# Expert rows gathered for two experts at a time, squares and roots of the expert norms one stage earlier, in a one-core forward pass

## The chip, the core and the metric

One core of a Trainium2 chip runs the whole program as a single launch. The metric is the device time of one execution in microseconds. The trace gives, for one execution, every instruction of the five engines (PE is TensorE, PEld its weight loads, DVE is VectorE, ACT is ScalarE, POOL is GpSimd) and every transfer, which SP (SyncE) issues except for a few.

## What is computed

Two networks follow each other on 256 tokens of width 1024, all in float32. The first block (mixer, memory attention, hierarchical experts) is not touched. The second has two layers. Layer 0 mixes with a state-space scan (SSD), layer 1 with attention, and each ends in an expert-choice stage:

```python
def moe_ec(h, router_w, w1, w3, w2):
    cap = EC_CAPACITY * T // N_EXPERTS_2
    aff = jax.nn.softmax(logits, axis=-1)
    gate, idx = lax.top_k(jnp.swapaxes(aff, 1, 2), cap)
    xg = h[bidx, idx]
    a = jnp.einsum('becd,edf->becf', xg, w1)
    g = jnp.einsum('becd,edf->becf', xg, w3)
    y = jnp.einsum('becf,efd->becd', jax.nn.silu(a) * g, w2)
    y = y * gate[..., None].astype(y.dtype)
    return jnp.zeros_like(h).at[bidx, idx].add(y.astype(h.dtype))
...
x = x + g2l * moe_ec(rmsnorm(x, norm2_w[i]) * (1.0 + sc2l) + sh2l, ...)
```

Each of 16 experts picks its 32 best rows (cap) of 256. Its three matrices are 1024 by 1024, so a layer reads 16 x 3 x 4 MB, some 201 MB. In layer 0 the tokens and a context of 256 rows go through the experts (two streams), in layer 1 the tokens alone. A last rmsnorm gives the output.

## The kernel before

The kernel is written out by hand: every engine has its own instruction list in each block, with semaphores between them, and a barrier of all five engines stands between blocks. A block is a stage: the SSD stage, the expert stage of layer 0 (tiles end in e or e0), the attention stage (5), the expert stage of layer 1 (e1). The two expert stages are one function, `expert_choice(l)`.

**Weights.** A list `stream` fixes the order in which SP issues the loads; SP takes them in that order and waits before each until the piece that held the buffer is used up (`piece.before.freed`). Buffers are six slots of 2 MB and extra tiles. An expert is six pieces of 2 MB (two halves each of w1, w3, w2). Layer 0 has 7 buffers (slots 0 to 5, `extra0`), layer 1 has 9 (two of them made of two tiles each, `extra1` with C and `extra2` with hT). In the SSD stage the slots also serve as scratch; all six become free with the last matmul of its output product (`scratch_use`), so the first pieces of layer 0 are issued there. In the attention stage four pieces of layer 1 are loaded while it runs, and five at or after its end.

**Front of an expert stage.** `NormT` normalises: ACT squares each tile of 128 rows with a row sum (`scalar_squares`), POOL makes the root of each (`pool`, `root`), DVE scales the tile (`vector_scale`), PE transposes it, DVE and ACT bring it to hT with gain and bias. Four tiles in layer 0, two in layer 1. Then come router logits, softmax, the choice of 32 rows by expert on DVE (`top8`), one-hot matrices (`mark`), and `fetch`: matmuls of the normalised rows (stationary, 128 x 128) with one-hot columns gather the chosen rows, transposed, into `xgT`. `take_unit` brings them out of PSUM. In layer 1 PE first runs four matmuls that only keep it busy, `hold(pe, 4)`.

**The expert loop.** `GROUP = 4`: rows are gathered for four experts at once, so a gather matmul has 4 x 32 = 128 moving columns. The first group is gathered in front of the loop; in each of experts 0 to 11 a quarter of the next group's gather follows the first product (`fetch(psum[2], ...)`), with ACT taking it out. PE's list for expert e is: two halves of w1 (line 2898), transposes of the gates, fetch, two halves of w3, scatter of the previous expert, transposes, two halves of w2.

Of the kernel before, what the change touches and what calls it, by code (L numbers as in the profile page):

```python
# [168 lines left out]
def build(nc, A, out):  # L169
# [15 lines left out]
    with ctx:  # L185
# [31 lines left out]
        dve_step, act_step, pool_step = sem("dve_step"), sem("act_step"), sem("pool_step")  # L217
# [116 lines left out]
        moe2_weights(0, (0, 1, 2, 3, 4, 5, SLOTS))  # L334
        ring.last[SLOTS + 1] = ring.last[SLOTS + 2] = extra_room[1]
        ring.last[SLOTS + 3] = extra_room[2]
        for n in (0, 1, 2):
            weights(("qkv", n), [(0, KD, 512, rows("attn_qkv_w_2")[:, :, n * 512:(n + 1) * 512])], (n + 5) % SLOTS)
        for n in range(2):
            weights(("attn_out", n), [(0, 4, D, rows("attn_out_w_2")[:, 4 * n:4 * n + 4, :])])  # L340
        moe2_weights(1, (4, 5, 0, 1, 2, 3, SLOTS + 1, SLOTS + 2, SLOTS + 3))
# [14 lines left out]


# [55 lines left out]
        counted = {"streams": 0, "norms": 0, "head_norms": 0, "ada": 0}  # L413

        class NormT:


            def __init__(self, tag, srcs, xn, hT, gain_col, bias_col=None, cols=None, apart=False, by=(DVE, ACTE)):
# [6 lines left out]
                counted["streams"] += self.T  # L425
                counted["norms"] += 1
# [6 lines left out]
            def pool(self, pool):  # L433
                for t in range(self.T):
                    pool.wait_ge(squared, self.before + t + 1)
                    root(pool, t, 1, D, rooted)

# [13 lines left out]
            def tensor(self, pe):  # L451
                m = self.per_bank()
                opened = [banks.open((self.tag, n), self.by[n % 2]) for n in range(KD // m)]
                for t in range(self.T):
                    pe.wait_ge(normed, self.before + t + 1)
# [1592 lines left out]
        with ExitStack() as ssd:  # L2048
            Yt_base = (nc.sbuf_base + 31) // 32 * 32
            Yt = sb("Yt", [P, 16, TT * P], scope=ssd)  # L2050
            Yt_r = nc.alloc_sbuf_tensor_at("Yt_r", [P, 16, TT * P], F32R, offset=Yt_base)
            rowsB = sb("rowsB", [P, 2, HPG, TT * P], scope=ssd)
            xst = sb("xst", [P, 2, 3, GW], scope=ssd)
# [31 lines left out]
            pos[0] = late + 2080  # L2085
            y_high_late = carve(8 * 512, flat_r).rearrange("p (c n) -> p c n", c=8)
            y_high = lambda i: h_high[:, i, :] if i < 8 else y_high_late[:, i - 8, :]
# [3 lines left out]
            g1 = rows_flat[:, 0:2048].rearrange("p (s n) -> p s n", s=2)  # L2091
            part = xst[:, :, :, :].rearrange("p d t n -> p (d t n)")[:, 0:1024].rearrange("p (a n) -> p a n", a=2)
# [45 lines left out]
            def _(pe):  # L2138
# [143 lines left out]

                sum_squares(6)
# [1068 lines left out]
```

## Time and profile before

| | us |
|---|---|
| median of 3 runs (2228.2 to 2230.95) | 2229.8 |
| the profiled execution, its own time | 2231.04 |
| its span in the trace | 2229.2 |
| PE busy | 2030.7 (91%) |
| DVE busy | 972.8 (44%) |
| ACT busy | 648.5 (29%) |
| POOL busy | 72.4 (3%) |
| 16 DMA queues, mean rate | 280 GB/s |

The mean over the span hides the stages. In the page's row of 40 slices (55.7 us each), the DMA rate is 427 or 428 GB/s in most slices of the two expert stages and 77 to 139 in the SSD stage. PE's granted clock is 0.977 of full speed in the mean.

### The profile page before, as it was taken

What the parts mean: (1) busy time and instruction counts of PE and PEld (TensorE: products, weight loads), DVE (VectorE), ACT (ScalarE), POOL (GpSimd) and SP (SyncE); (2) the same over time, 40 slices, a digit from 0 to 9 for tenths busy, and PEclk for the clock granted to TensorE, in tenths of its full rate; (3) what the DMA queues carried; (4) which work ended last, traced back from release to release, by engine and by line L of the source; (5) the groups of instructions that cost most, each with busy time, mean ns of one, the idle gap of its engine ahead of it and who ended that gap; (6) DMA issues with size and microseconds to landing.
All of it is one profiled execution on the core that took longest, in us unless ns stands there. A gap on an engine that the chain in (4) does not pass through costs nothing. (4 is left out here: it accounts for less than half of the span.)

```text
span 2229.2 us, 25119 instructions
## 1 busy us (share of the span) xinstructions
PE 2030.7 (91%) x10198; PEld 1076.0 (48%) x10198; DVE 972.8 (44%) x1668; ACT 648.5 (29%) x1284; POOL 72.4 (3%) x106
## 2 busy tenths in 40 slices
PE   6987988999899999999899999988899899999887
PEld 5844444444377888878643333322445422222222
DVE  4687224444688889882522221222466400011002
ACT  4244023111276667762211111100226111111000
POOL 0101010000000000000100000000120000000000
PEclk9999998999999999999999999999999999999999
DMA  8637477899333433322489999999820599999997
GB/s 289 214 139 277 176 266 294 339 388 384 111 97 98 139 105 114 114 96 77 186 360 429 427 428 427 427 428 428 328 110 1 211 427 427 424 427 426 427 425 301
DMA packets 147177, 623.58 MB, mean 280 GB/s; under 512 B 15443, under 2 KB 66134, under 8 KB 109046
## 3 DMA queue, kind: packets, MB, share of 16 engines
q1 hardware_dynamic: 142144, 601.65, 67.8%
q0 software_dynamic: 2352, 16.91, 1.9%
q10 hardware_dynamic: 2566, 3.41, 0.5%
q8 instruction: 82, 1.34, 0.2%
q14 instruction: 33, 0.27, 0.0%
HBM read 620.76 MB, written 1.18 MB: 279 GB/s over the span
## 5 line engine op out<-in xcount | busy, mean ns | idle before, releaser
L2898 PE MATMUL bank<-slots,xgTe 128*64 128x512 f32 (+1 forms) x1584 | 355.0, 595 | 30.4 <-DMA slots<-in_moe_w 30.3
L3119 DVE TENSOR_TENSOR actse<-sge,bank 32x512 f32<-32x512 f32 (+1 forms) x48 | 32.8, 682 | 499.2 <-PE bank L2898 278.4
L2898 PEld LDWEIGHTS bank<-slots,xgTe 128*64 128x64 f32 (+1 forms) x1584 | 102.7, 125 | 259.5 <-issue 216.2
L2898 PE MATMUL bank<-slots,aTe 128*64 128x512 f32 (+1 forms) x800 | 188.4, 615 | 18.3 <-issue 18.3
L514 PE MATMUL bank<-slots_r 128*128 128x512 f32 x512 | 201.2, 393 | 0.0
L3016 ACT ACTIVATE sge<-bank 32x512 f32<-32x512 f32 (+1 forms) x48 | 28.3, 590 | 481.5 <-PE bank L2898 481.3
L513 PE MATMUL bank<-hT_r,slots_r 128*128 128x512 f32 x384 | 155.6, 405 | 0.0
L515 PE MATMUL bank<-slots_r 128*128 128x512 f32 x384 | 152.0, 396 | 0.0
L583 PE MATMUL bank<-slots,hT 128*128 128x512 f32 (+1 forms) x320 | 133.2, 578 | 4.6 <-DVE hT L480 3.0
L2898 PEld LDWEIGHTS bank<-slots,aTe 128*64 128x64 f32 (+1 forms) x800 | 55.3, 128 | 130.8 <-issue 130.8
L514 PEld LDWEIGHTS bank<-slots_r 128*128 128x128 f32 x512 | 96.3, 188 | 22.6
L3028 ACT ACTIVATE aTe<-bank 128x512 f32<-128x512 f32 x32 | 19.1, 597 | 275.4 <-PE bank L2955 275.4
L583 PEld LDWEIGHTS bank<-slots,hT 128*128 128x128 f32 x320 | 61.7, 194 | 74.5 <-issue 66.9
L2493 DVE SCALAR_TENSOR_TENSOR slots<-slots,vcols 128x512 f32<-128x512 f32 x128 | 95.5, 751 | 4.0 <-ACT slots L2345 0.3
L1690 PE MATMUL bank<-slots,hT 128*64 128x512 f32 x368 | 88.4, 615 | 9.6 <-ACT hT L1802 4.9
L2133 DVE TENSOR_TENSOR slots_r<-slots,slots_r 128x2048 fp32r<-128x2048 f32 x32 | 73.1, 2286 | 42.4 <-ACT slots_r L2128 42.2
L515 PEld LDWEIGHTS bank<-slots_r 128*128 128x128 f32 x384 | 72.2, 188 | 17.7
L513 PEld LDWEIGHTS bank<-hT_r,slots_r 128*128 128x128 f32 x384 | 72.1, 188 | 16.8 <-issue 1.2
L2362 ACT ACTIVATE rowsB<-rowsB,nb 128x128 f32<-128x128 f32 x256 | 76.5, 391 | 2.2 <-DVE rowsB L2619 2.2
L362 POOL TENSOR_SCALAR rstd<-eps_rows 128x1 f32<-128x1 f32 (+5 forms) x41 | 17.6, 430 | 1796.9 <-ACT xn L430 624.3
L2128 ACT ACTIVATE slots_r<-slots 128x2048 fp32r<-128x2048 f32 x32 | 61.0, 1906 | 51.1 <-PE bank L515 51.1
L2898 PE MATMUL bank<-extra0e,xgTe 128*32 128x512 f32 (+1 forms) x304 | 68.8, 594 | 4.5 <-DMA extra0e<-in_moe_w 4.5
(561 smaller groups left out, 3099.0 us busy)
## 6 DMA issues: line engine op xcount, KB each, us to landing
slots<-in_moe_w SPq DMA_DIRECT2D x149, 2048.0 KB, 26.5
slots<-in_ada_w SPq DMA_DIRECT2D x24, 2048.0 KB, 12.2
extra0e<-in_moe_w SPq DMA_DIRECT2D x23, 2048.0 KB, 26.5
slots<-in_ssd_in_w SPq DMA_DIRECT2D x48, 512.0 KB, 5.3
slots<-in_moe_w_gate SPq DMA_DIRECT2D x23, 1024.0 KB, 10.6
slots<-in_moe_w_up SPq DMA_DIRECT2D x23, 1024.0 KB, 12.6
slots<-in_moe_w_down SPq DMA_DIRECT2D x23, 1024.0 KB, 7.3
rowsB<-acum_rows POOLq DMA_DIRECT2D x16, 1024.0 KB, 5.8
```

The lines of the kernel that those rows point to most:

```text
L513: pe.matmul(out, lhsT[0], rhs[1], start=start, stop=False, skip_group_check=True)
L514: pe.matmul(out, lhsT[0], rhs[0], start=False, stop=False, skip_group_check=True)
L515: return pe.matmul(out, lhsT[1], rhs[0], start=False, stop=stop, skip_group_check=True)
L583: i = pe.matmul(b.ap[:, 0:width], lhsT(k), rhs(k), start=(k == 0), stop=(k == K - 1))
L1690: i = pe.matmul(b.ap[j * CAP1:(j + 1) * CAP1, :].rearrange("p (m n) -> p m n", m=2), xg[:, p // 2 % 2, k, at:at + CAP1], piece.ap.rearrang ...
L2128: act.activation(high_half(w), raw_half(w), ACT.Copy).then_inc(w_rounded, 1)
L2133: dve.tensor_tensor(low_half(w), raw_half(w), high_half(w).bitcast(F32), ALU.subtract).then_inc(w_split, 1)
L2362: i = act.activation(r, r, ACT.Exp, bias=nb[:, t, col:col + 1])
L2493: i = dve.scalar_tensor_tensor(o, padded[:, c, :, j:j + S], tap(j, CH(g)[c]), o, ALU.mult, ALU.add)
L2898: i = pe.matmul(bank[64 * n:64 * n + NJ * CAP, :], lhsT(4 * h + k), wv[:, 0, n * 512:(n + 1) * 512], start=(h == 0 and k == 0), stop=(h == ...
L3016: i = act.activation(sg[r_, :], psum[0][r_, :], ACT.Silu)
L3119: i = dve.tensor_tensor(acts[r_, :], sg[r_, :], psum[1][r_, :], ALU.mult)
```

## The change

`GROUP` goes from 4 to 2 in both layers, so a gather matmul has 64 moving columns and each gather takes twice as many of them for the same rows; fourteen experts carry a share of the next group's gather, where twelve did. The squares and roots of the expert norms move to the end of the block in front (`early_squares`, `early_roots`, with a third POOL instruction for the factor of 32). The scaling is shared: DVE takes the even tiles of a stream and ACT the odd ones (`shared_scale`). Layer 0 has a norm for each stream. Scratch of the SSD stage moves out of slots 3 to 5, so that three pieces of layer 0 may be loaded before the output product ends; the order of buffers is changed with it. In layer 1 one buffer lies where the attention's queries were and is free once these are transposed; `fin`, the last norm's gain, has a tile of its own.

```diff
@@ end_scratch, group_scratch, gate_scratch
-        scratch_use = Piece(None, None, 0, None)
+        group_scratch, gate_scratch, end_scratch = (Piece(None, None, 0, None) for _ in range(3))
         for slot in range(SLOTS):
-            ring.last[slot] = scratch_use
+            ring.last[slot] = (end_scratch, end_scratch, end_scratch, gate_scratch, group_scratch, group_scratch)[slot]
...
-        moe2_weights(0, (0, 1, 2, 3, 4, 5, SLOTS))
-        ring.last[SLOTS + 1] = ring.last[SLOTS + 2] = extra_room[1]
+        moe2_weights(0, (5, 4, 3, 0, 1, 2, SLOTS))
+        ring.last[SLOTS + 1] = extra_room[1]
...
-        moe2_weights(1, (4, 5, 0, 1, 2, 3, SLOTS + 1, SLOTS + 2, SLOTS + 3))
+        queries_room = Piece(None, None, 0, None)
+        ring.last[SLOTS + 2] = queries_room
+        moe2_weights(1, (1, 2, 5, 4, SLOTS + 2, 3, 0, SLOTS + 1, SLOTS + 3))
...
+        def stream_root(pool, t, done):
+            link = chain(pool, pool_step)
+            c = slice(t, t + 1)
+            link(pool.tensor_scalar(rstd[:, c], eps_rows[:, c], float(D * EPS), None, ALU.add))
+            link(pool.tensor_tensor(rstd[:, c], rstd[:, c], minus_half[:, 0:1], ALU.pow))
+            pool.tensor_scalar(rstd[:, c], rstd[:, c], float(D) ** 0.5, None, ALU.mult).then_inc(done, 1)
+        def early_squares(act, junk, tiles):
+            for t, src in enumerate(tiles):
+                act.wait_ge(stream_added, counted["added"] + 1)
+                if t:
+                    act.wait_ge(squared, counted["streams"] + t)
+                counted["added"] += 1
+                act.activation(junk, src, ACT.Square, accum_out=eps_rows[:, t:t + 1]).then_inc(squared, 1)
+        def early_roots(pool, n):
+            for t in range(n):
+                pool.wait_ge(squared, counted["streams"] + t + 1)
+                stream_root(pool, t, rooted)
...
+            def shared_scale(self, eng, by):
+                for t, src in enumerate(self.srcs):
+                    if (t % 2 == 0) != (by == DVE):
+                        continue
+                    eng.wait_ge(rooted, self.before + t + 1)
+                    dst = self.xn[:, t, :].rearrange("p (h j m) -> p h m j", h=2, j=4)
+                    src = src.rearrange("p (h m j) -> p h m j", h=2, j=4)
+                    r = rstd[:, self.at + t:self.at + t + 1]
+                    if by == DVE:
+                        eng.tensor_scalar(dst, src, r, None, ALU.mult).then_inc(normed, 1)
+                    else:
+                        eng.activation(dst, src, ACT.Copy, scale=r).then_inc(act_normed, 1)
...
-            GROUP = 4
+            GROUP = 2
...
-                norm = NormT(tag, [r for rs in res for r in rs], xn, hT, segs, apart=True)
+                norms = [NormT(f"{tag}s{j}", res[j], xn[:, NT * j:NT * (j + 1), :], hT[:, :, S * j:S * (j + 1)], segs_of(j),
+                               at=NT * j, shared=True) for j in range(NJ)]
...
-                    norm.pool(pool)
...
-                    norm.scalar_squares(act)
-                    norm.evacuate(act, ACTE)
+                    for norm in norms:
+                        norm.shared_scale(act, ACTE)
+                    for norm in norms:
+                        norm.evacuate(act, ACTE)
```

ACT at the border between the SSD stage and the expert stage of layer 0, before (C and X are the two streams, the UNCONDITIONAL_BRANCH rows are the border):

```order
L2382 ACTIVATE slots_r<-Yt,vcols 128x512 x2
L2048 UNCONDITIONAL_BRANCH
L2993 UNCONDITIONAL_BRANCH [waits barrier_Pool_Activation_PE_DVE_SP_release]
L430 ACTIVATE xne,eps_rows<-C 128x1024 x2
L430 ACTIVATE xne,eps_rows<-X 128x1024 x2
L484 ACTIVATE hT<-bank,modcol,ncol 128x256 [waits bank_full]
```

The same place on ACT in the changed kernel:

```order
L2440 ACTIVATE hT_r<-Yt,vcols 128x512 x2
L376 ACTIVATE hp,eps_rows<-C 128x1024 [waits stream_added]
L376 ACTIVATE hp,eps_rows<-C 128x1024 [waits squared,stream_added]
L376 ACTIVATE hp,eps_rows<-X 128x1024 [waits squared,stream_added] x2
L2101 UNCONDITIONAL_BRANCH
L3060 UNCONDITIONAL_BRANCH [waits barrier_Pool_Activation_PE_DVE_SP_release]
L481 ACTIVATE xne<-C,rstd 128x2x128x4 [waits rooted]
L481 ACTIVATE xne<-X,rstd 128x2x128x4 [waits rooted]
L537 ACTIVATE hT<-bank,modcol,ncol 128x256 [waits bank_full]
```

The four squares now stand ahead of the border, the last of them behind the last addition to the streams, and two scalings stand behind it.

PE in expert 0 of layer 0, before: the product with w1 (from xgTe), the gate transposes (gcure), the gather for the next group (from hT and xne, into one PSUM bank), the product with w3:

```order
L2898 MATMUL bank<-slots,xgTe 64x512 [waits slot_loaded1,emptied_by_act,emptied_by_dve]
L2898 MATMUL bank<-slots,xgTe 64x512 x7
L2937 MATMUL bank<-consts,gcure 128x128 [waits emptied_by_act,gc_ready_e0]
L2937 MATMUL bank<-consts,gcure 128x128
L2871 MATMUL bank<-hT,xne 128x128 [waits onehot_ready_e0,emptied_by_dve]
L2871 MATMUL bank<-hT,xne 128x128 x7
L2898 MATMUL bank<-slots,xgTe 64x512 [waits slot_loaded2,emptied_by_act]
```

The same place on PE in the changed kernel:

```order
L2966 MATMUL bank<-slots,xgTe 64x512 [waits slot_loaded4,emptied_by_act,emptied_by_dve]
L2966 MATMUL bank<-slots,xgTe 64x512 x7
L3005 MATMUL bank<-consts,gcure 128x128 [waits emptied_by_act,gc_ready_e0]
L3005 MATMUL bank<-consts,gcure 128x128
L2939 MATMUL bank<-hT,xne 128x64 [waits onehot_ready_e0,emptied_by_dve]
L2939 MATMUL bank<-hT,xne 128x64 x15
L2966 MATMUL bank<-slots,xgTe 64x512 [waits slot_loaded3,emptied_by_act]
```

Eight gather matmuls of 128 columns became sixteen of 64, between the same neighbours.

## Rows read from the trace of the kernel before

**Rows 1.** Windows: stretch, length, busy us of each engine, PE clock, DMA share, GB/s

```profile
1091.00:1134.00 43.00, 31.94 (x189) 21.86 (x190) 27.43 (x67) 14.84 (x30) 5.60 (x8) 0.88 0.83 342
...
1500.00:1560.00 60.00, 51.05 (x242) 16.84 (x238) 12.68 (x20) 3.73 (x10) 0.00 (x0) 1.00 1.01 428
...
1700.00:1750.00 50.00, 45.84 (x192) 23.14 (x188) 19.36 (x52) 14.05 (x34) 0.00 (x0) 1.00 0.00 1
```

**Rows 2.** Timeline of PE, experts of layer 0: start us, us, what, idle before

```profile
1130.06 7.09 PE L2898 MATMUL bank<-slots,xgTe 128*64 128x512 f32 x32
...
1345.12 3.60 PE L2898 MATMUL bank<-extra0e,xgTe 128*64 128x512 f32 x16
1349.60 3.65 PE L2898 MATMUL bank<-slots,xgTe 128*64 128x512 f32 x16 [0.87 <-DMA slots<-in_moe_w]
...
1577.20 3.65 PE L2898 MATMUL bank<-slots,aTe 128*64 128x512 f32 x16
```

**Rows 3.** Timeline of SP's issues of weight loads

```profile
1057.75 0.37 SPq L354 DMA_DIRECT2D slots<-in_ssd_out_w  x1
...
1091.19 3.01 SPq L354 DMA_DIRECT2D slots<-in_moe_w  x6
...
1133.75 24.09 SPq L354 DMA_DIRECT2D slots<-in_moe_w  x6
...
1749.34 0.81 SPq L354 DMA_DIRECT2D slots<-in_moe_w  x2
...
1778.78 22.13 SPq L354 DMA_DIRECT2D slots<-in_moe_w  x6
```

**Rows 4.** Timeline of all engines, front of the expert stage of layer 0

```profile
1092.04 0.69 DVE L2732 TENSOR_TENSOR X<-X,xst 128x512 f32<-128x512 f32 x1
1094.63 1.06 ACT L430 ACTIVATE xne<-C 128x1024 f32<-128x1024 f32 x1 [22.53 <-PEq L2048]
...
1096.17 0.57 POOL L363 TENSOR_TENSOR rstd<-rstd,minus_half 128x1 f32<-128x1 f32 x1
...
1098.14 4.79 PE L460 MATMUL bank<-consts,xne 128*128 128x128 f32 x24 [6.98 <-DVE xne L445]
...
1102.00 1.34 DVE L445 TENSOR_SCALAR xne<-X,rstd 128x1024 f32<-128x1024 f32 x1 [0.33 <-POOL rstd L363]
1103.40 1.09 PE L460 MATMUL bank<-consts,xne 128*128 128x128 f32 x8 [0.46 <-DVE xne L445]
...
1121.09 9.04 PE L2871 MATMUL bank<-hT,xne 128*128 128x128 f32 x64 [1.30 <-DVEq L3093]
```

**Rows 5.** The same timeline, front of the expert stage of layer 1

```profile
1750.14 0.69 DVE L3316 TENSOR_TENSOR X<-X,part 128x512 f32<-128x512 f32 x1
...
1751.37 3.67 PE L509 MATMUL bank<-consts 128*128 128x512 f32 x8 [2.07 <-PEq L3173]
...
1756.84 1.10 PE L460 MATMUL bank<-consts,xne 128*128 128x128 f32 x8 [0.91 <-DVE xne L445]
```

**Rows 6.** Timeline of PE: a gather of layer 0, a 32-column matmul elsewhere, and their successors

```profile
1137.35 1.95 PE L2871 MATMUL bank<-hT,xne 128*128 128x128 f32 x16
1139.23 7.09 PE L2898 MATMUL bank<-slots,xgTe 128*64 128x512 f32 x32
```

```profile
627.48 1.97 PE L2254 MATMUL bank<-slots,consts 128*128 128x32 f32 x16
629.29 0.68 PE L2259 MATMUL bank<-slots,consts 128*128 128x256 f32 x2
```

**Rows 7.** PE behind an earlier border of blocks: its timeline, and the window

```profile
1589.25 3.13 PE L2042 MATMUL bank<-consts,modcol 128*128 128x128 f32 x16 [1.91 <-PEq L2755]
```

```profile
1590.00:1592.00 2.00, 2.00 (x12) 2.00 (x10) 0.63 (x1) 2.00 (x5) 1.29 (x3) 0.50 1.03 400
```

**Rows 8.** Timeline of PE, experts 11 and 15 of layer 1

```profile
2074.06 3.63 PE L2898 MATMUL bank<-slots,xgTe 128*32 128x512 f32 x16 [1.18 <-DMA slots<-in_moe_w]
...
2201.75 3.63 PE L2898 MATMUL bank<-slots,xgTe 128*32 128x512 f32 x16 [1.17 <-DMA slots<-in_moe_w]
```

More of the change, by code:

```diff
@@ L454, in tensor @@
                 for t in range(self.T):
-                    pe.wait_ge(normed, self.before + t + 1)
+                    self.wait_normed(pe, t)
                     for n, b in enumerate(opened):
@@ L2281, in _ @@
                     outputs(g)
+                group_scratch.freed = (emptied[DVE], banks["y", SSD_G - 1, 1].done)
                 sum_squares(6)
@@ L2286, in _ @@
                 sum_squares(7)
+                gate_scratch.freed = (bank_full, banks["ss", 7].full)
                 outs = [(t, n, banks.open(("so", t, n), DVE)) for t in range(TT) for n in range(2)]
@@ L2311, in _ @@
                     half(w).freed = (gate_full, q + 1) if q < 7 else (bank_full, b.full)
-                scratch_use.freed = (bank_full, b.full)
+                end_scratch.freed = (bank_full, b.full)
             @block.gpsimd
@@ L2825, in _ @@
                         hold(pe, 4)
-                    norm.tensor(pe)
+                    for norm in norms:
+                        norm.tensor(pe)
                     pe.wait_ge(wide_ready, 1)
@@ L2994, in _ @@
                 def _(act):
-                    norm.scalar_squares(act)
-                    norm.evacuate(act, ACTE)
+                    for norm in norms:
+                        norm.shared_scale(act, ACTE)
+                    for norm in norms:
+                        norm.evacuate(act, ACTE)
                     act.wait_ge(sub_ready, 1)
@@ L3040, in _ @@
                     dve.tensor_copy(wide[:, :, 0:N_EXP], wr).then_inc(wide_ready, 1)
-                    norm.vector_scale(dve)
-                    norm.evacuate(dve, DVE)
+                    for norm in norms:
+                        norm.shared_scale(dve, DVE)
+                    for norm in norms:
+                        norm.evacuate(dve, DVE)
                     b = banks[tag, "quarters"]
@@ L3198, in build @@
             q_ready, k_ready = sem("q5_ready"), sem("k5_ready")
+            X_tiles = [X[:, t, :] for t in range(NT)]
             to_qT = Transpose("qT5", lambda n, t: q[:, t, n * P:(n + 1) * P], QH // 2, P, lambda g, m: qT[:, g:g + m, :])
@@ L3239, in _ @@
                 to_qT.wait_all(pe)
+                queries_room.freed = (bank_full, banks["qT5", to_qT.groups()[-1][0]].full)
                 for g in (KVH - 2, KVH - 1):
```

77 lines of the change are left out of this document (53 added, 24 removed).

## The prediction

> **What bounds the kernel now.** I read the stages by window first, since the means of the page mix them. In the expert stages the transfers run at 428 GB/s with the engines' share at 1.01, and a few stretches are poor: the last 50 us of attention move 1 GB/s, and the 43 us between the end of the SSD stage and the first used piece of layer 0 move 342 [rows 1]. So transfers bound the expert stages, and what counts is when they start to run without a gap.
>
> The timeline of SP's issues says when. In layer 0 seven pieces go out at and just after 1091.19, the eighth at 1133.75, when expert 0 has used its first piece [rows 3]. Seven pieces at 4.91 us each (2.10 MB at 427 GB/s) end near 1127, so the transfers then stand still for some 7 us: the window's 43 x (1 - 342/427) = 8.6 us says the same. In layer 1 the steady stream starts at 1778.78, again with the first freed buffer [rows 3]. I call these two moments the starts. **All buffers are full at both starts**, before as after, so a start depends on the chain norm, router, choice, gather, and not on how early the first pieces came.
>
> The timeline of PE tells the rest. From expert 0 at 1130.06 to expert 8 at 1345.12 PE runs without a wait for a transfer: 26.88 us per expert. The first such wait comes at 1349.60, and the last product ends at 1577.20 + 3.65 = 1580.85 [rows 2], 450.8 us after expert 0 began. Six pieces take 6 x 4.91 = 29.5 us. So PE has 2.6 us per expert in hand, no more. In layer 1 it reaches the transfers only in expert 11 [rows 8].
>
> **The sum, term by term.**
>
> *A, front of layer 0: -2.9 us.* The last addition ends at 1092.04 + 0.69 = 1092.73, ACT's first square starts at 1094.63 [rows 4]: the barrier waited for SP, whose six issues end at 1091.19 + 3.01 = 1094.20 [rows 3], and then took 0.4. Now three of the six are issued near 1058, behind the last load of the SSD stage [rows 3], and the other three end by 1092.7. But the last square (1.06 and 0.19 for the read of the sum) and three POOL instructions (two like the 0.57 one at most [rows 4], one of some 0.2, with 0.1 between) now stand ahead of the barrier: 1092.8 + 1.25 + 1.1 + 0.4 = 1095.6, a border 1.0 later. Behind it DVE scales two tiles in place of four, ACT two beside it (a row of ACT's square, the same size, takes 1.06), so both end near 1099 where DVE ended at 1102.00 + 1.34 = 1103.34. PE becomes the limit: 24 transposes took 4.79 at the lower clock, eight 1.09 [rows 4]; 32 from 1097.6 end near 1103.1 against 1104.49. The first stream is brought to hT meanwhile, so the half of that work which came after the last transpose goes: together 2.6 earlier. The one-hot marks for two experts in place of four save some 0.3. The first gather has the same 64 records [rows 4]; at 64 columns they cost what they did (term B), so nothing there. Bounds: 0 (ACT slow on its permuted writes, or the low clock for longer) and -4.4: the first gather's 64 records took 9.04 [rows 4], where 64 at the steady 0.118 of term B are 7.5, so 1.5 more if it now runs at full clock throughout.
>
> *B, experts of layer 0: +1.8 us.* The gather of an expert is 16 records (a float32 matmul leaves two) in 1139.23 - 1137.35 = 1.88 us, 0.118 each with 128 columns. The nearest narrow row has 32 columns and the same full stationary: 16 in 629.29 - 627.48 = 1.81, 0.113 each [rows 6]. A quarter of the columns saves 4%, so 64 columns save nothing to speak of and 16 more records cost 1.85 us per expert. PE's own pace becomes 26.88 + 1.85 = 28.73 for fourteen experts and 25.0 for the two without a gather: 452.2 us, against the 450.8 that transfers allowed. The transfers themselves: the third piece of expert 0 was freed 9.05 us after the start; now 10.9, and two pieces take 9.8, so they wait 1.1 once. The two limits lie within half a microsecond of each other, +1.4 and +1.1; where both bind by turns the end comes a little behind either, hence +1.8. Bounds: +1.1 (PE never late) and +6 (0.3 us more per expert over fourteen: a stretch of lower clock or a wait for ACT, which now takes out eight small blocks where it took four).
>
> The Trainium skill (TensorE: Matmul & The Clock Gate, section "Back-to-back issue gap") gives the gap of an isolated warm matmul as moving columns over 2.4 GHz plus 2.5 ns, by which half the columns would be nearly half the price and the gather would cost no more than before. Its section on LDWEIGHTS ties the weight load to the stationary's columns, which stay 128, and the rows here side with that one. By the first, B would be +0 and the sum of all terms near zero or below; by the rows it is +1.8.
>
> *Attention stage: 0.* It keeps its instructions; ACT and POOL are idle where squares and roots go, except behind the last addition. Its weights follow the same pieces as before. One more piece (4.9 us of transfer) comes in during the 50 us that move nothing [rows 1]. That work would show only if the start waited for transfers: of its nine pieces five are issued from 1749.34 on [rows 3], 24.6 us of transfer, which end near 1774, ahead of the start at 1778.78; now four of them do.
>
> *C, front of layer 1: +2.5 us.* Here the barrier waited for the last addition alone: 1750.83, PE's next matmul at 1751.37 [rows 5]. Square and root now stand between, 1.25 + 1.1 + 0.1 = 2.4 us. Behind the border PE must first run the four holding matmuls, 3.67 us; they lay beside squares, roots and scaling, and that cover is gone. Transposes of the second tile began at 1756.84; now 1751.37 + 2.4 + 3.67 + 1.05 = 1758.5, 1.65 later [rows 5]. PE also idles 4.5 us there where it idled 2.07. Behind another border it idled 1.91 us and the next 2 us had the clock at 0.50, that is 1.2 GHz of 2.4 [rows 7]; a spell of that in the holding matmuls can cost at most 1.85, half of what runs in it, and I take 1.0. Marks save 0.15. Bounds: +1.5 and +3.6.
>
> *D, experts of layer 1: +0.3 us.* One stream, so eight more records, 0.92 us per expert, on a PE that waits from expert 11 on. It came to expert 11's second piece at 2074.06 - 1.18 = 2072.9 [rows 8], 294.1 after the start, 26.7 per expert. With 0.92 more in eleven experts it comes there after 304.2; four experts on, less 1.0 for the one without a gather and with 0.92 in three, after 412.9; and at expert 15's fourth piece 7.3 later (two pieces of 3.5 and the gate transposes), after 420.2. That piece was there 2201.75 - 1778.78 = 423.0 after the start [rows 3, 8]. PE is still first, by 3 us, so transfers decide. Bounds 0 and +3.4 (low-clock spells in most experts).
>
> Sum: -2.9 + 1.8 + 2.5 + 0.3 = +1.7 us. From the profiled execution's 2231.04 that is 2232.7; it lies 1.2 above the median of its runs, so for a median I give 2229.8 + 1.7 = **2231.5 us**.
>
> **The rivals.**
> *PE becomes the bound of layer 0 (slower).* For it: 2.6 us in hand against 1.85 spent, and every 0.1 us more per expert is 1.4 us at the end. If a gather record costs what the first gather's did, 9.04/64 = 0.141, the gather takes 4.5 us where I have 3.7: 14 x 0.8 = +11, 2243. It decides from about 0.25 us per expert. Against it: that mean has a low clock in it, and the steady row is 0.118. With milder forms and C and D near their upper bounds it has a chance of 0.25.
> *Narrow gathers are half price (faster).* B falls away, the first gather loses up to 4 us in layer 0 and 1.9 in layer 1: -6.9 + 0 + 0.6 + 0 = -6.3, 2223.5. The 32-column row speaks against it. Chance 0.07; it is what the first of the two rules would give.
> *The early loads count (faster).* If starts waited for transfers, three pieces and one piece would give 4 x 4.9 = 19.6 us: 2210. The 7 us and 3 us without transfers before the starts speak against it. Chance 0.04.
>
> **How the numbers follow.** A measurement of this kernel can tell about 0.2%, 4.5 us, from no change. My case has 0.64 and lies within it, as 2231.5 is 0.08% up. All its lower bounds together give -4.4 + 1.1 + 1.5 = -1.8 us, 2228, all its upper ones 0 + 6 + 3.6 + 3.4 = +13, 2242.8. The range goes a little below the first, towards the faster rivals, and leaves out the upper third, since those bounds would have to meet: 2226 to 2238. Faster 0.12, same 0.63, slower 0.25.
>
> **What would show it.** Right: POOL's last root of each early norm ends ahead of the border, the border of layer 1 comes 2.4 us after the last addition and not 0.5; 32 gather records per expert of layer 0 take 3.7 us; PE's wait for transfers in layer 0 first comes in expert 12 or later, or hardly at all; layer 0 ends 450 to 454 us after expert 0 starts; transfers stand still longer before both starts than now. Wrong: gather records at 0.06 to 0.08 us, or an expert 0 in layer 0 that begins much sooner than 33 us after its border (it was 1130.06 - 1094.63 = 35.4 [rows 2, 4]). The prediction fails upwards if PE's pace in layer 0 exceeds 29 us per expert.

## The result, and the profile after

The changed kernel takes 2247.9 us (median of 5 runs, 2246.8 to 2248.3) where the kernel before takes 2231.0 beside it: a ratio of 1.0079, 95% interval 1.0069 to 1.0090. It is slower, by 17 us. The forecast was 2231.5 with a range up to 2238, so it was wrong: the measured time lies 10 us above the range.

The profiled executions stand 17.2 us apart as well (spans 2246.4 and 2229.2), so the stages can be set side by side. A "start" is, as in the prediction, the moment of the issue into the first freed buffer; "front" is what lies between the last addition of the stage ahead and the start.

| us | before | after | difference | forecast |
|---|---|---|---|---|
| up to the last addition of the SSD stage | 1092.7 | 1094.2 | +1.5 | 0 |
| front of layer 0 | 41.0 | 45.3 | +4.3 | A: -2.9 |
| experts of layer 0, start to last product | 447.1 | 449.0 | +1.9 | B: +1.8 |
| attention, to its last addition | 170.0 | 170.6 | +0.6 | 0 |
| front of layer 1 | 28.0 | 35.5 | +7.5 | C: +2.5 |
| experts of layer 1 | 437.9 | 439.1 | +1.3 | D: +0.3 |

The first row is no effect: over the fourteen profiled executions of this case that addition ended anywhere between 1089.8 and 1095.4. Nearly the whole miss is in the two fronts, and inside them in one place:

| us | layer 0, before / after | layer 1, before / after |
|---|---|---|
| last addition to border | 1.9 / 4.2 | 0.5 / 2.8 |
| border to end of the router's product | 14.1 / 9.9 | 8.8 / 9.4 |
| from there to the first gather | 12.4 / 12.1 | 11.2 / 11.1 |
| first gather to the start | 12.7 / 19.1 | 7.4 / 12.3 |

The last row holds +6.5 and +4.9 us, 11.3 of the 17.2, and the forecast had nothing there. PE's timeline of the changed kernel, around the two first gathers (start us, us, what, idle before it):

```profile
1112.66 5.32 PE L562 MATMUL bank<-consts 128*128 128x512 f32 x12
1119.01 0.31 PE L2933 MATMUL bank<-consts,ye0e 32*128 32x32 f32 x2 [1.03 <-DVEq L3149]
1120.40 13.92 PE L2939 MATMUL bank<-hT,xne 128*128 128x64 f32 x64 [1.08 <-DVEq L3164]
1134.25 8.68 PE L2966 MATMUL bank<-slots,xgTe 128*64 128x512 f32 x32
...
1143.13 2.12 PE L2939 MATMUL bank<-hT,xne 128*128 128x64 f32 x18
...
1761.99 5.37 PE L562 MATMUL bank<-consts 128*128 128x512 f32 x8 [4.27 <-PEq L3243]
...
1782.38 6.89 PE L2939 MATMUL bank<-hT,xne 128*128 128x64 f32 x32 [0.74 <-DVEq L3164]
1789.20 8.86 PE L2966 MATMUL bank<-slots,xgTe 128*32 128x512 f32 x32
```

As many records, 64, as took 9.04 before [rows 4] take 13.92, that is 0.217 each, where at 1143.13 the same instruction takes 0.118 (2.12 us for 18 records). The first expert product behind it takes 8.68 in place of 7.09 [rows 2]. The windows of the changed kernel say why (stretch, length, busy us of PE, PE's weight loads, DVE, ACT, POOL, then the granted clock, DMA share, GB/s):

```profile
1118.00:1120.00 2.00, 0.31 (x2) 0.20 (x2) 1.40 (x7) 0.00 (x0) 0.00 (x0) 1.00 0.00 0
1120.00:1122.00 2.00, 1.60 (x8) 1.60 (x8) 0.92 (x7) 0.00 (x0) 0.00 (x0) 0.61 0.04 12
1122.00:1124.00 2.00, 2.00 (x11) 2.00 (x11) 0.00 (x0) 0.00 (x0) 0.00 (x0) 0.50 0.00 0
...
1132.00:1134.00 2.00, 2.00 (x11) 2.00 (x10) 2.00 (x5) 0.00 (x0) 0.00 (x0) 0.50 0.00 0
1134.00:1136.00 2.00, 2.00 (x6) 0.66 (x7) 1.85 (x5) 1.65 (x6) 0.00 (x0) 0.50 0.00 0
1136.00:1138.00 2.00, 2.00 (x8) 0.62 (x6) 0.55 (x2) 1.32 (x2) 0.00 (x0) 0.63 0.00 0
1138.00:1140.00 2.00, 2.00 (x12) 0.70 (x10) 0.00 (x0) 0.00 (x0) 0.00 (x0) 1.00 0.00 0
```

PE is almost idle from 1118 to 1120.4, and from about 1120.4 the granted clock is 0.50, 1.2 GHz of 2.4. It stays there through the whole gather, although PE is busy for 2.00 of every 2.00 us, and returns at 1137.5, in the product of 512 columns. In layer 1 the low stretch around the gather runs from about 1782.6 to 1792.9. In the kernel before the clock was low for some 3.4 us of the first gather in layer 0, and around that of layer 1 not at all. Its windows in layer 0:

```profile
1122.00:1124.00 2.00, 2.00 (x13) 2.00 (x12) 0.20 (x2) 0.00 (x0) 0.00 (x0) 0.58 0.98 418
1124.00:1126.00 2.00, 2.00 (x12) 2.00 (x12) 1.19 (x4) 0.00 (x0) 0.00 (x0) 0.57 0.99 418
1126.00:1128.00 2.00, 2.00 (x20) 2.00 (x20) 0.00 (x0) 1.41 (x4) 0.00 (x0) 1.00 0.67 279
```

What answers to the other rows of before: the issues of SP (three of the six go out early inside the second row's 34 us, the other three from 1092.71),

```profile
1059.12 0.37 SPq L357 DMA_DIRECT2D slots<-in_ssd_out_w  x1
1059.53 34.46 SPq L357 DMA_DIRECT2D slots<-in_moe_w  x6
1098.37 0.33 SPq L357 DMA_DIRECT2D extra0e<-in_moe_w  x1
1139.54 3.76 SPq L357 DMA_DIRECT2D slots<-in_moe_w  x2
```

and PE in the experts of layer 0, with its first wait for a transfer, and the window that stood for this stage:

```profile
1564.33 3.65 PE L2966 MATMUL bank<-slots,xgTe 128*64 128x512 f32 x16 [1.15 <-DMA slots<-in_moe_w]
...
1584.92 3.65 PE L2966 MATMUL bank<-slots,aTe 128*64 128x512 f32 x16
```

```profile
1500.00:1560.00 60.00, 58.53 (x303) 21.96 (x301) 15.44 (x25) 6.20 (x18) 0.00 (x0) 1.00 1.01 427
```

PE's busy time in that window went from 51.05 [rows 1] to 58.53 of 60, and its first wait for a transfer from expert 8 to expert 15: this stage is bound by PE and by transfers at once, as forecast, and in this pair of executions it cost what was forecast (1.9 us against 1.8; run 11 has the mean over all).

### The profile page after: what moved, and what is told of

It is laid out like the page before. It is cut to its first block and busy times, and to the rows that moved or that the text cites. A ratio compares the mean times of both kernels' runs of the same rounds, so it can differ in the third digit from the quotient of the medians.

```text
span 2246.4 us, 26007 instructions
## 1 busy us (share of the span) xinstructions
PE 2072.1 (92%) x10582; PEld 1127.4 (50%) x10582; DVE 967.5 (43%) x1665; ACT 680.7 (30%) x1383; POOL 71.4 (3%) x112
## 3 DMA queue, kind: packets, MB, share of 16 engines
HBM read 620.76 MB, written 1.18 MB: 277 GB/s over the span
## 5 line engine op out<-in xcount | busy, mean ns | idle before, releaser
L2966 PE MATMUL bank<-slots,xgTe 128*64 128x512 f32 (+1 forms) x1664 | 373.4, 598 | 9.3 <-DMA slots<-in_moe_w 9.3
L2966 PEld LDWEIGHTS bank<-slots,xgTe 128*64 128x64 f32 (+1 forms) x1664 | 107.9, 125 | 247.4 <-issue 233.7
L2966 PE MATMUL bank<-slots,aTe 128*64 128x512 f32 (+1 forms) x704 | 160.1, 596 | 13.9 <-issue 13.9
L3085 ACT ACTIVATE sge<-bank 32x512 f32<-32x512 f32 (+1 forms) x48 | 28.3, 590 | 463.7 <-PE bank L2966 463.5
L567 PE MATMUL bank<-slots_r 128*128 128x512 f32 x416 | 163.5, 393 | 0.0
L568 PE MATMUL bank<-slots_r 128*128 128x512 f32 x384 | 152.0, 396 | 0.0
L2966 PEld LDWEIGHTS bank<-slots,aTe 128*64 128x64 f32 (+1 forms) x704 | 47.5, 127 | 110.0 <-issue 110.0
L2939 PE MATMUL bank<-hT,xne 128*128 128x64 f32 x768 | 98.9, 291 | 1.8 <-DVEq L3164 1.8
L2939 PEld LDWEIGHTS bank<-hT,xne 128*128 128x128 f32 x768 | 97.7, 209 | 2.0 <-DVEq L3164 2.0
L3097 ACT ACTIVATE aTe<-bank 128x512 f32<-128x512 f32 x32 | 19.1, 597 | 239.6 <-PE bank L3023 239.6
L567 PEld LDWEIGHTS bank<-slots_r 128*128 128x128 f32 x416 | 78.3, 188 | 18.1
L3048 ACT ACTIVATE xgTe<-bank,modcol,ncol 128x64 f32<-128x64 f32 x180 | 56.5, 409 | 83.6 <-PE bank L2939 83.6
L568 PEld LDWEIGHTS bank<-slots_r 128*128 128x128 f32 x384 | 72.3, 188 | 17.7
L566 PE MATMUL bank<-slots_r,hT_r 128*128 128x512 f32 (+1 forms) x192 | 74.8, 390 | 3.6 <-DVE hT_r L1121 3.6
## 6 DMA issues: line engine op xcount, KB each, us to landing
slots<-in_ada_w SPq DMA_DIRECT2D x24, 2048.0 KB, 12.7
```

Source lines behind the costliest of these rows:

```text
L566: pe.matmul(out, lhsT[0], rhs[1], start=start, stop=False, skip_group_check=True)
L567: pe.matmul(out, lhsT[0], rhs[0], start=False, stop=False, skip_group_check=True)
L568: return pe.matmul(out, lhsT[1], rhs[0], start=False, stop=stop, skip_group_check=True)
L2939: i = pe.matmul(bank[:, u * W:(u + 1) * W], xn[:, j * NT + t, k * P:(k + 1) * P], onehot[:, t, j, g * W:(g + 1) * W], start=(t == 0), stop ...
L2966: i = pe.matmul(bank[64 * n:64 * n + NJ * CAP, :], lhsT(4 * h + k), wv[:, 0, n * 512:(n + 1) * 512], start=(h == 0 and k == 0), stop=(h == ...
L3048: return eng.activation(dst, src, ACT.Identity, scale=gain, bias=bias)
```

## The experiments

The theory formed from these rows: **narrow start**. The pause of PE ahead of the first gather lets the clock fall; the 128-column matmuls of a gather bring it back after a while, 64-column ones do not; the 512-column product must do it. Rivals: the pause (or its moment) alone decides and the columns do not matter; the early squares and roots are what costs; the early loads matter after all.

The readings of all runs in one table. "Gathers" are the durations of the two first gathers; fronts and experts as above, all from one profiled execution of each kernel; the ratio is to the kernel before in the same session. In layer 0 runs 4, 6 and 7 are the same kernel, and front 0 is 37.0, 38.5 and 37.3: by that much a front differs without a cause in the kernel.

| run | gathers | front 0 | front 1 | experts 0 | experts 1 | median | ratio (95%) |
|---|---|---|---|---|---|---|---|
| before | 9.04, 3.84 | 41.0 | 28.0 | 447.1 | 437.9 | 2231.0 | |
| changed | 13.92, 6.89 | 45.3 | 35.5 | 449.0 | 439.1 | 2247.9 | 1.0079 (1.0069 to 1.0090) |
| 1 wide first | 8.78, 5.37 | 38.7 | 32.2 | 450.4 | 438.6 | 2236.8 | 1.0036 (1.0018 to 1.0053) |
| 2 group of four | 9.04, 5.47 | 40.6 | 32.4 | 447.0 | 441.1 | 2237.3 | 1.0026 (1.0013 to 1.0039) |
| 3 before, group of two | 12.30, 4.72 | 45.9 | 31.1 | 450.1 | 442.2 | 2242.5 | 1.0056 (1.0037 to 1.0074) |
| 4 hold between | 7.36, 3.68 | 37.0 | 30.5 | 449.7 | 439.2 | 2235.2 | 1.0026 (1.0013 to 1.0039) |
| 5 late slots | 7.36, 3.68 | 38.5 | 30.4 | 450.3 | 439.4 | 2235.0 | 1.0021 (1.0009 to 1.0033) |
| 6 norm 1 late | 7.36, 3.68 | 38.5 | 28.3 | 448.7 | 439.2 | 2233.3 | 1.0010 (1.0000 to 1.0019) |
| 7 hold moved | 7.36, 3.68 | 37.3 | 27.7 | 449.0 | 442.1 | 2231.9 | 1.0000 (0.9990 to 1.0009) |
| 8 before, hold | 7.41, 3.81 | 39.4 | 27.9 | 445.8 | 441.9 | 2229.6 | 0.9992 (0.9981 to 1.0002) |
| 9 root 3 late | 7.36, 3.68 | 35.8 | 27.6 | 449.8 | 441.9 | 2229.7 | 0.9993 (0.9980 to 1.0005) |
| 10 warm, two | 7.36, 3.68 | 35.2 | 27.6 | 448.7 | 442.3 | 2230.9 | 0.9996 (0.9986 to 1.0005) |
| 11 warm, four | 7.41, 3.81 | 35.6 | 27.8 | 445.7 | 437.9 | 2225.8 | 0.9974 (0.9961 to 0.9986) |
| 12 norms late, four | 7.41, 3.82 | 38.1 | 28.7 | 447.0 | 440.0 | 2231.6 | 1.0008 (0.9999 to 1.0017) |

**1. Only the first gather wide.** It multiplies by the marks of four experts and hands on two.

```
-                        fetch(b.ap, 0, units).then_inc(bank_full, 1)
+                        fetch(b.ap, 0, units, 4 * CAP).then_inc(bank_full, 1)
...
-                    mark(0, GROUP)
+                    mark(0, 4)
```

> The changed kernel, but the first gather of either layer, and it alone, multiplies by 128 one-hot columns (four experts) and hands on the 64 that are wanted: the same number of records, twice the columns. Theory 'narrow start' (a run of 64-column matmuls behind the pause does not bring the clock back up, one of 128 columns does): the first gathers take 9.0 and 3.9 us in place of 13.92 and 6.89, the first expert product 7.1 in place of 8.68 and 8.86, some 10 us less in all: 2238. Rival 'pause ahead' (what lies ahead of the gather, or luck, sets the clock and the columns do not matter): the gathers stay above 12 and 6 us, the time 2248. Rival 'marks' (the wait for the marks of four experts is what narrow gathers save): at most 0.3 us, seen as a later start of the gather.

Measured 2236.8, and the gathers took 8.78 and 5.37. The first gather of layer 0 by timeline, and its windows:

```profile
1119.70 8.78 PE L2939 MATMUL bank<-hT,xne 128*128 128x128 f32 x64 [1.34 <-DVEq L3164]
1128.41 7.09 PE L2966 MATMUL bank<-slots,xgTe 128*64 128x512 f32 x32
```

```profile
1120.00:1122.00 2.00, 2.00 (x11) 2.00 (x10) 0.36 (x3) 0.00 (x0) 0.00 (x0) 0.50 0.04 8
1122.00:1124.00 2.00, 2.00 (x17) 2.00 (x17) 0.84 (x4) 0.00 (x0) 0.00 (x0) 0.85 0.00 0
1124.00:1126.00 2.00, 2.00 (x21) 2.00 (x20) 0.26 (x2) 1.06 (x4) 0.00 (x0) 1.00 0.00 0
```

The two traces compare well: at clock 0.50 either kernel gets 11 records into 2 us and PE is busy for all of it, so pace, busy time and number of matmuls agree while the clock is low. Only the columns differ, and with twice the columns the clock is back within about 3 us, where with half of them it did not come back before the gather ended. In layer 1 it gave back 3.3 of 4.9, since there the wide gather met a low stretch too, which the profiled kernel before had not. Together 9.9 us by the fronts, as the theory said.

One execution could be luck, but the other traces agree. Five gathers of 128 columns met a fallen clock (layer 0 of the kernel before, both layers of runs 1 and 2), and each time it was back inside the gather, 3.4 us after it fell. Four gathers of 64 columns met one (both layers of the changed kernel and of run 3), and it never came back before the gather's end: the low stretches last 6.8 to 17.1 us. So the rival on the pause alone is refuted. The number of columns is not all that counts, though: the 32 transposes behind the border of layer 0 have 128 columns too, and PE ran them at 0.50 for 5.8 us in run 5 and 6.0 in run 6. What it is in a matmul that raises the clock is not shown.

**2. Four experts at a time again,** the rest of the change kept (`GROUP = 4`, and the gain of the last norm back in half of the gathered rows).

> The changed kernel with rows gathered for four experts at a time again, in both layers; early squares and roots, shared scaling and early loads stay. Theory 'narrow start': the 10 us of the starts come back, and the 1.9 and 1.3 us of the two expert stages: 2248 - 13 = 2235, and what is left of +4 over the kernel before is the border of layer 1 (+2.3) with the holding matmuls at the low clock (+1.7), less what the front of layer 0 gains (-4.2 + 2.3). Rival 'the early norms cost it' (moving squares and roots is what made it slow): above 2243.

2237.3, within 2.3 of the theory. The first gather and the experts of layer 0 are those of before again. What is left is front 1 (with 1.6 us in its gather, 5.47 in place of 3.84, which met a low stretch of 3.4 us), and 3.2 us in the experts of layer 1, where PE waits for transfers anyway and the executions differ by as much without a cause in the kernel (437.9 to 442.3 in the table).

**3. The kernel before with two experts at a time.** The same edit the other way (the gain gets its own buffer).

> The kernel before with two experts at a time in place of four (the gain of the last norm gets a buffer of its own, since it no longer fits in half of the gathered rows; its load comes at the same moment), and nothing else of the change. Theory 'narrow start': the first gathers go from 9.04 and 3.84 us towards 14 and 7, and the experts of layer 0 and 1 grow by 1.9 and 1.3: 2231 + 5 + 3 + 1.6 + 3 = 2244. Rival 'early norms cost it': 2231 + 3 = 2234, with the first gathers as they were.

2242.5. By the ratios the narrow gather alone costs 12 of the 17 us, and the rest of the change (run 2) about 6; added up, about the 17 of the whole. In layer 0 its first gather began at full clock, which fell 1.8 us later and stayed low for the other 10.5. In layer 1 the clock fell only near 1781, well into the gather, so the gather itself took no more than 4.72, and the product behind it paid instead:

```profile
1778.16 4.72 PE L2871 MATMUL bank<-hT,xne 128*128 128x64 f32 x32 [0.74 <-DVEq L3093]
1782.81 9.43 PE L2898 MATMUL bank<-slots,xgTe 128*32 128x512 f32 x32
```

So where the low stretch begins, and whether there is one, differs from one profiled execution to the next; how long it lasts depends on what runs in it.

**4. One holding matmul in the pause.**

```
+                    hold(pe, 1)
                     pe.wait_ge(onehot_ready, 1)
                     for n, units in FIRST:
```

> The changed kernel with one more holding matmul (two records of 512 columns, 0.44 us each at full clock) in the pause between the small transposes and the first gather of either layer. Theory 'narrow start' in its strict form (narrow matmuls let the clock fall wherever they run) says that the gathers stay near 13.9 and 6.9 us: 2248. Its milder form (they do not raise a low clock, but keep a high one) and the rival 'pause ahead' say that with the pause filled the clock stays high: gathers of 7.3 and 3.7 us, 2238.

2235.2. PE's timeline and a window inside the gather:

```profile
1116.60 0.31 PE L2933 MATMUL bank<-consts,ye0e 32*128 32x32 f32 x2 [1.04 <-DVEq L3150]
1116.84 1.12 PE L562 MATMUL bank<-consts 128*128 128x512 f32 x2
1117.99 7.36 PE L2939 MATMUL bank<-hT,xne 128*128 128x64 f32 x64
```

```profile
1120.00:1122.00 2.00, 2.00 (x20) 2.00 (x19) 1.10 (x4) 0.19 (x1) 0.00 (x0) 1.00 0.00 0
```

Behind a filled pause the narrow gather keeps the full clock: 64 records in 7.36 us, 0.115 each, and the same in every later run with two at a time. In run 3 it began at full clock as well, but behind an open pause, and lost it; so the pause brings the fall, and in these gathers the columns decide how long it lasts. The strict form of the theory falls; the milder one holds. One matmul (two records) in a pause of 1.1 us gives back what the narrow gather lost at both starts.

**5. Without the early loads of layer 0** (all six slots wait for the end of the stage in front).

```
-            ring.last[slot] = (end_scratch, end_scratch, end_scratch, gate_scratch, group_scratch, group_scratch)[slot]
+            ring.last[slot] = end_scratch
```

> The changed kernel with the one holding matmul in the pause (as in the run of that name), and here without the early loads of layer 0: all six buffers wait for the end of the stage in front, as before the change. Theory 'starts wait for the chain, not for transfers': the time stays that of the kernel with the holding matmul, 2235, since all pieces are there before expert 0 anyway. Rival 'the early loads count': three pieces of 4.9 us come back as a loss, 2240 to 2250. It also looks at the border of layer 0, which came 1.7 us after POOL's last root where layer 1 took 0.3: if SP's early issues have a hand in it, it falls towards 0.4 here; if not it stays 1.7.

2235.0 against 2235.2: the early loads are worth nothing that can be measured here, where the rival had 5 us or more. The border comes 1.72 us after POOL's last root ended, as with the early loads, so SP has no part in it.

**6. Squares and roots of layer 1 back behind the border.** In this kernel the norm of layer 1 lacks its constant factor of 32, the square root of the width, and with it one POOL instruction of some 0.25 us per tile.

> The changed kernel with the one holding matmul in the pause, and squares and roots of layer 1 back behind the border of its expert stage, as in the kernel before; the scaling stays shared by DVE and ACT, layer 0 stays as changed. Theory of term C: the border comes 2.3 us sooner after the last addition, the holding matmuls run beside squares and roots and at more than the low clock again; from last addition to first freed piece 27 us in place of 30.5, the whole 3 to 3.5 us less than with the holding matmul alone, about 2232. Rival 'the norms are cheap wherever they stand' (they are only shifted from one side of the border to the other): 2235.

2233.3, and front 1 fell from 30.5 to 28.3 (27 was expected). The border comes 0.3 after the last addition in place of 2.8. What is missing to the 27 is in part ACT's scaling of the second tile: PE waits 1.66 us for it, where in the kernel before it waited 0.91 for DVE's [rows 5]. Early squares and roots are a loss in layer 1 as they stand, of 2.2 us by these two fronts, and of 1.8 against the 28.7 of run 12, which has the whole norm behind the border.

**7. The holding matmuls of layer 1 moved.**

```
@@ end of the attention, PE
+                hold(pe, 5)
@@ front of the expert stage, PE
-                        hold(pe, 4)
+                        hold(pe, 1)
```

> The changed kernel with the one holding matmul in the pause; squares and roots of layer 1 stay early, but of the four holding matmuls at the front of layer 1 one stays and five (ten records, 4.4 us at full clock) run behind the last product of the attention, beside the last addition, square and root. Theory 'lost cover': transposes then wait only for the scaling, 2.2 us behind the border in place of 5.1, at full clock: 2.9 us less than with the holding matmul alone, 2232, and from last addition to first freed piece 27.5 us. Rival 'the clock falls at the border all the same': the transposes at the low clock (16 records of 0.24 in place of 0.12) eat 1.5 to 2 of it, 2234.

2231.9 and a front of 27.65, both within 0.2 of the theory. PE at the border:

```profile
1745.95 4.45 PE L562 MATMUL bank<-consts 128*128 128x512 f32 x10
1750.70 1.10 PE L562 MATMUL bank<-consts 128*128 128x512 f32 x2 [0.30 <-PEq L3244]
```

The ten records run at 0.44 each beside the last addition, square and root, where eight took 5.37 us behind the border in the changed kernel. The idle time there falls from 4.27 to 0.30, and the router's product ends 6.1 us behind the border in place of the 9.3 of run 4. The cover that was lost can be had again by moving what was covered.

**8. The kernel before with one holding matmul in its pause.**

> The kernel before with one holding matmul in the same pause ahead of the first gathers, and nothing of the change. Theory: its first gather of layer 0 has a stretch at the low clock too (9.04 us for 64 records); with the pause filled it takes 7.6, that of layer 1 stays at 3.8: 1.4 us less, 2229, hardly told apart from 2230.6 by the times, but seen in the records. Rival 'only narrow gathers profit': the gather stays at 9.0 and the time at 2230.6.

2229.6. The gather fell from 9.04 to 7.41 and front 0 from 41.0 to 39.4, as expected; the ratio's interval (0.9981 to 1.0002) does not tell it from no change.

**9. The fourth root of layer 0 behind the border.**

```
-                early_roots(pool, TT)
+                early_roots(pool, TT - 1)
...
+                    if l == 0:
+                        pool.wait_ge(squared, norms[0].before + T)
+                        stream_root(pool, T - 1, rooted)
```

> The kernel with the holding matmul in the pause and the moved holding matmuls of layer 1, and here the root of the fourth tile of layer 0 stands behind the border on POOL; its square and the other three roots stay early. It asks what the 1.7 us are between POOL's last root (end 1096.65) and the border of layer 0 (1098.37). Theory 'POOL is late by itself' (the end of POOL's part costs it 1.7 more behind the last root): POOL's last early root now ends near 1094.3, so the border comes with 1094.3 + 1.7 or with ACT's last square + 0.4, both near 1096 on the clock of the profiled changed kernel, 2.4 us sooner after the last addition (1.8 in place of 4.2), and the whole is up to 2 us faster than with the moved holding matmuls, 2230. Rival 'something else holds the border' (DVE, PE or SP): it stays 4.2 behind the last addition, 2232.

2229.7, and the border comes 1.8 after the last addition in place of 4.2, as expected. The timeline of all engines at the border:

```profile
1094.74 0.69 DVE L2791 TENSOR_TENSOR X<-X,xst 128x512 f32<-128x512 f32 x1
...
1094.88 0.64 POOL L367 TENSOR_SCALAR rstd<-rstd 128x1 f32<-128x1 f32 x1
1095.46 1.06 ACT L376 ACTIVATE hp<-X 128x1024 f32<-128x1024 f32 x1 [1.62 <-DVE X L2791]
1096.43 0.19 ACT L376 ACTIVATION_READ_ACCUMULATOR hp<-X 128x1 f32 x1
1097.23 0.33 SPq L357 DMA_DIRECT2D extra0e<-in_moe_w  x1
1097.26 2.08 ACT L481 ACTIVATE xne<-C,rstd 128x1024 f32<-128x1024 f32 x1 [0.65 <-PEq L2101]
1097.28 0.21 POOL L365 TENSOR_SCALAR rstd<-eps_rows 128x1 f32<-128x1 f32 x1 [1.76 <-POOLq L2101]
...
1097.57 2.62 POOL L366 TENSOR_TENSOR rstd<-rstd,minus_half 128x1 f32<-128x1 f32 x1
...
1097.82 1.22 DVE L479 TENSOR_SCALAR xne<-C,rstd 128x1024 f32<-128x1024 f32 x1
1098.83 1.32 DVE L479 TENSOR_SCALAR xne<-X,rstd 128x1024 f32<-128x1024 f32 x1
```

POOL's root ends at 1095.52 and the border is at 1097.24: 1.72, as in the changed kernel and in runs 1, 2 and 4 to 7. But ACT's square ends only 0.62 ahead of it, so here the square may have set it too; that POOL holds the border in the changed kernel follows from the 2.4 us that moving one root saved.

The moved root has a price of its own. Its second instruction takes 2.62 us where it takes 0.57 ahead of the border, and it ends 0.04 us behind the second of DVE's two scalings. Runs 10 and 11 show the same (2.62 and 2.70, ends 0.04 and 0.03 behind DVE's), and beside a single scaling of DVE in the kernel before POOL's instructions take 1.2 to 1.3. So on this evidence POOL's instruction waits for DVE's scalings, and ACT's second scaling for POOL.

**10 and 11. PE kept busy over the border of layer 0 as well** (three holding matmuls behind the last product of the SSD stage, two ahead of the transposes), with two experts at a time and with four.

> As the run before it, and PE kept busy over the border of layer 0 too: three holding matmuls behind the last product of the SSD stage and two in front of the transposes. Still two experts at a time. Theory (a pause drops the clock, and what runs behind it pays): the 32 transposes take 3.9 to 4.3 us in place of 5.0 and end up to 1.5 sooner, held by ACT's scaling (4.1 us behind the border); 1 us less, 2229. Rival 'the scaling sets the end anyway': no change, 2230.

> As the run before it, but four experts at a time: everything of the change but the narrow gather, with PE kept warm. Theory of terms B and D: 1.9 and 1.3 us of the expert stages come back, 3 us less than with two at a time: 2226, faster than the kernel before by 0.2%. Rival 'the transfers swallow it' (layers end with the transfers whatever PE does): 1 us or less, 2228.

Run 10 took 2230.9, no gain over run 9: front 0 is 0.6 shorter, and the scaling sets the end, as the rival had it. Its timeline of PE and ACT:

```profile
1095.24 2.84 PE L513 MATMUL bank<-consts,xne 128*128 128x128 f32 x24
1098.83 1.09 PE L513 MATMUL bank<-consts,xne 128*128 128x128 f32 x8 [0.75 <-ACT xne L481]
```

```profile
1096.68 2.09 ACT L481 ACTIVATE xne<-X,rstd 128x1024 f32<-128x1024 f32 x1 [1.18 <-POOL rstd L367]
```

The transposes run at full clock (24 in 2.84 us), but the last eight wait for ACT's second scaling, and that waited 1.18 us for the root that run 9 put behind the border, slowed beside DVE's scalings as said there.

Run 11 took 2225.8, ratio 0.9974 (0.9961 to 0.9986), the only version faster than the kernel before. Between these two only the group differs: 3.0 us in the experts of layer 0 and 4.4 in those of layer 1. The first is what the whole table says (experts 0 with four: 446.5 on average over five executions, with two: 449.5 over nine). The second is mostly the spread named under run 2: over the same executions experts 1 take 439.8 and 440.4. The profiled execution of run 11 is one of its fastest, 3.4 us under its median.

**12. Run 11 with squares and roots of both layers behind the borders.**

> The kernel with four experts at a time and PE kept warm, but the squares and roots of both layers back behind the borders, in ACT and POOL of the expert stages; scaling shared, holding matmuls in the pause, four in front of the transposes of both layers, early loads kept. It asks what the early squares and roots are worth by themselves. Theory: in layer 0 four squares (1.05 us each on ACT) and the last root (1.1) stand again ahead of the last scaling (2.0), 7.5 us of chain behind a border that comes 1.3 sooner than with them early; from last addition to first freed piece 38 us in place of 35.6. In layer 1 27.9 in place of 27.8. In all 2 to 2.5 us more than the kernel with them early: 2228. Rival 'all the gain is the clock' (holding matmuls and shared scaling do it alone): 2226.

2231.6 where 2228 was expected. Front 0 is 38.1 (38 expected) against 35.6, front 1 28.7 against 27.8; that is 3.4 us for the early squares and roots once POOL's last root and the holding matmuls stand right. The two medians are from different sessions and stand 5.8 us apart (7.6 by the ratios); the rest lies outside the fronts (experts 1.2 and 2.1 longer in the profiled executions), and what it comes from was not found.

## Why the prediction was wrong

**The step that failed** is in term A: "The first gather has the same 64 records [rows 4]; at 64 columns they cost what they did (term B), so nothing there", and with it the bound "so 1.5 more if it now runs at full clock throughout". Term C had no word on the gather at all, and its only spell of low clock was in the holding matmuls. The steady rows of term B [rows 6] are rows at full clock. The first gather stands behind a pause of over a microsecond, and its own 9.04 us had "a low clock in it", as the rival on PE's pace says in so many words. I used that row to bound a gain, as if the low stretch were a fixed sum that could only be lost or kept, and did not ask what ends it. The runs showed in its place: with 128 columns the clock comes back during the gather, with 64 it does not (run 1 against the changed kernel), and with the pause filled neither pays (runs 4 and 8). The gathers took 13.92 and 6.89 us in place of 9.04 and 3.84, and with the product behind them it cost 6.5 and 4.9 us.

**Term A otherwise.** Border +1.0 forecast, +2.3 measured: I let the last root be followed by 0.4 us, as SP's issue had been, and in this place the border comes 1.72 behind it. Behind the border 3.6 forecast (2.6 and the 1.0), 4.2 measured, with ACT's scaling at 2.08 and not at the 1.06 of its square: a wrong price that lay within the forecast bound and hid behind the transposes. Without the gather A would have been -2.2.

**Term B**, +1.8: +1.9 from start to last product, PE's pace 28.56 us per expert (forecast 28.73), its first wait in expert 15 ("expert 12 or later, or hardly at all"). The first of the two rules of the Trainium skill weighed there (TensorE: Matmul & The Clock Gate, "Back-to-back issue gap") would have made the 32 narrow records half as dear; they took 3.68 us, 0.115 each, against 0.118 at 128 columns, so the trace sides with the section on LDWEIGHTS, as the prediction had it. Over all executions of the table the group is worth 3.0 in this stage: 1.2 more than the term, and within its bounds, so that the 1.9 of the one pair came so near the forecast is in part luck.

**Attention**, 0: +0.6.

**Term C**, +2.5: +7.5. The border (+2.3 of 2.4) and the holding matmuls without cover and at the low clock (5.37 in place of 3.67, 1.7 where I took 1.0 of a possible 1.85) came as described. Without the gather it is +2.7. **Term D**, +0.3: +1.3, inside its bounds and inside the spread of that stage.

**The rivals.** "PE becomes the bound of layer 0" had the right sign and the wrong place: its own price, a gather record of 0.141 or more, did come, at 0.217, but only in the first gather of each layer, where it does not repeat 14 times. "Early loads count" is refuted by run 5, "narrow gathers are half price" by every steady record. The missing rival was one sentence long: the first gathers meet a fallen clock, and narrow matmuls may not raise it. At the low clock the two cost 64 x 0.217 = 13.9 and 32 x 0.217 = 6.9 us, +4.9 and +3.1, before the product behind them; the low clock inside the gather of before was there to be asked about.

**Where the expected gain went.** The early squares and roots, with the shared scaling, do shorten the path behind the border of layer 0 by 4.2 us. The later border gives back 2.3, layer 1 loses 2.7 by them, narrow records cost 1.9 and 1.3 in the experts, and the low clock around the first gathers 11.3. Run 11 mends the border, the cover and the clock and undoes the narrow gather; it is 0.26% faster than the kernel before.

## What to carry to other kernels

A matmul behind a pause can have two prices, and the clock that fell need not come back while it runs: read the granted clock of the stretch in which it runs, ask which instruction will raise it, and be wary of making that very instruction narrower. If a pause of a microsecond cannot be closed, a wide dummy matmul in it can be worth several times its length: 1.12 us of it took 8.2 us off the stretch from the first gather to the start in layer 0 of the changed kernel (run 4), and 1.6 us in the kernel before (run 8). And where idle or dummy work on one engine covers a chain on others, a chain that moves across a barrier must take its cover along.

## What the runs showed of the hardware that was not expected

- Float32 matmuls of 64 columns with a full stationary, issued without a gap (PE busy 2.00 of 2.00 us, 11 records in each), left the granted clock at 0.50 for as long as they ran (13.9 us in layer 0); in the same gathers with 128 columns it was at 1.00 again 3.4 us after its fall, five times of five. With the pause ahead of them filled the narrow ones stayed at 1.00 for 7.36 us and ran at 0.115 per record. Transposes of 128 columns ran at 0.50 for up to 6.0 us (run 6). Why is not shown.
- ACT's scaling of a 128x1024 tile with its permuted write took 2.08 us where its square of the same size took 1.06; DVE took 1.20 to 1.36 for the same scaling. Whether the order of the write makes the difference was not tested.
- Behind POOL's last early root the border of layer 0 came 1.72 us later (root end 1096.65, SP's issue 1098.37 in the changed kernel; the same in runs 1, 2 and 4 to 7), that of layer 1 only 0.30 later (1761.64 and 1761.94). What happens in the 1.72 is open.
- POOL's 128x1 instruction of 0.57 us took 2.62 to 2.70 us beside two of DVE's scalings and ended 0.03 to 0.04 us behind the second (runs 9, 10 and 11).
